# One TRN2 core, a two-part transformer in fp32: where a stage's squares are summed, and where beta is applied

## What is computed

```
def rms_norm(x, w):
    y = x32 * lax.rsqrt(jnp.mean(x32 * x32, axis=-1, keepdims=True) + EPS)
    return (y * w.astype(jnp.float32)).astype(x.dtype)

def gated_delta_rule(q, k, v, g, beta):
    decay = jnp.cumsum(g, axis=-1)
    rel = jnp.exp(jnp.where(causal, decay[..., :, None] - decay[..., None, :], -jnp.inf))
    k_beta = k * beta[..., None]
    a = jnp.where(strict, jnp.einsum('bhnik,bhnjk->bhnij', k_beta, k) * rel, 0.0)
    rhs = jnp.concatenate([v * beta[..., None], k_beta * jnp.exp(decay)[..., None]], axis=-1)
    sol = lax.linalg.triangular_solve(eye + a, rhs, left_side=True, lower=True, unit_diagonal=True)
    ...

def first_block(...):
    for l in range(DEPTH):
        ...
        h = h + rms_norm(xa, norm_xattn_post[l])
        hn = rms_norm(h, norm_ffn_pre[l])
        h = h + rms_norm(swiglu_ffn(hn, w_gate_up[l], w_down[l]), norm_ffn_post[l])
    return h
```

## Time and profile before

| | us |
|---|---|
| median of 3 runs | 2617.42 |
| lowest, highest | 2612.06, 2617.83 |
| the profiled execution's own time | 2612.81 |
| its span in the trace | 2610.9 |
| PE busy | 2529.0 (97%) |
| DVE busy | 1645.3 (63%) |
| ACT busy | 1128.4 (43%) |

### The profile page before, as it was taken

How to read it: one execution, slowest core, us unless ns; L and a number is a source line. 1 busy time by engine, 2 the same in 40 slices (tenths; PEclk the granted TensorE clock), 3 DMA queues, 4 the chain that set the end, 5 groups by cost and what they waited for, 6 DMA issues and landing times.

```text
span 2610.9 us, 34979 instructions
## 1 busy us (share of the span) xinstructions
PE 2529.0 (97%) x13470; PEld 2048.0 (78%) x13470; DVE 1645.3 (63%) x3123; ACT 1128.4 (43%) x2051; POOL 0.2 (0%) x4
## 2 busy tenths in 40 slices
PE   8999999999999999999999999999999999999998
PEld 6878888678888878788986788888876666888666
DVE  6666565364446776665653644478486677499774
ACT  4336444443332243464444433333336667232563
POOL 0000000000000000000000000000000000000000
PEclk9999999999999999999999999999999999999999
DMA  4220043123336522201421222375110000232321
GB/s 164 88 73 17 17 129 105 57 69 109 97 97 224 178 73 93 65 9 41 131 89 62 84 97 98 97 257 174 43 52 14 24 17 17 65 85 64 82 55 49
DMA packets 74083, 219.38 MB, mean 84 GB/s; under 512 B 21312, under 2 KB 21568, under 8 KB 73152
## 3 DMA queue, kind: packets, MB, share of 16 engines
q1 hardware_dynamic: 48384, 176.29, 20.9%
q10 hardware_dynamic: 25536, 40.87, 5.1%
HBM read 215.03 MB, written 2.10 MB: 83 GB/s over the span
## 4 chain that ended last, share of the span: by engine, by line
PE 87%; DVE 7%; ACT 3%; issue 2%; ACTq 0%; DVEq 0%
PE bank L579 21%; PE bank L580 21%; PE bank L581 21%; PE bank L796 4%; PE bank L832 4%; PE bank L806 3%; PE bank L1406 1%; DVE w_lo L545 1%; PE bank L1393 1%; PE bank L698 1%; PE bank L610 1%; PE bank L611 1%; PE bank L612 1%; DVE e_s L897 1%; DVE hT L767 1%
## 5 line engine op out<-in xcount | busy, mean ns | idle before, releaser
L579 PE MATMUL bank<-a_hi,w_hi 128*128 128x512 f32 (+1 forms) x1480 | 591.9, 400 | 19.9 <-DVE w_lo L545 14.5
L538 ACT ACTIVATE w_hi<-w_raw 128x1024 fp32r<-128x1024 f32 x334 | 353.4, 1060 | 562.2 <-PE bank L581 534.2
L581 PE MATMUL bank<-a_hi,w_lo 128*128 128x512 f32 (+1 forms) x1480 | 577.8, 390 | 0.0
L580 PE MATMUL bank<-a_lo,w_hi 128*128 128x512 f32 (+1 forms) x1480 | 577.1, 390 | 0.0
L545 DVE TENSOR_TENSOR w_lo<-w_raw,w_hi 128x1024 fp32r<-128x1024 f32 x334 | 407.7, 1223 | 264.5 <-ACT w_hi L538 263.8
L579 PEld LDWEIGHTS bank<-a_hi,w_hi 128*128 128x128 f32 (+1 forms) x1480 | 276.9, 187 | 88.5 <-issue 14.5
L581 PEld LDWEIGHTS bank<-a_hi,w_lo 128*128 128x128 f32 (+1 forms) x1480 | 276.6, 187 | 60.5
L580 PEld LDWEIGHTS bank<-a_lo,w_hi 128*128 128x128 f32 (+1 forms) x1480 | 277.0, 187 | 57.8 <-issue 1.4
L579 PE MATMUL bank<-b_hi,w_hi 128*128 128x512 f32 x704 | 257.2, 365 | 1.0 <-DVE w_lo L545 0.8
L580 PE MATMUL bank<-b_lo,w_hi 128*128 128x512 f32 x704 | 248.7, 353 | 0.0
L581 PE MATMUL bank<-b_hi,w_lo 128*128 128x512 f32 x704 | 247.5, 352 | 0.0
(11 more groups left out here) (393 smaller groups left out, 3959.2 us busy)
## 6 DMA issues: line engine op xcount, KB each, us to landing
w_raw<-w_tiles SPq DMA_DIRECT2D x334, 512.0 KB, 3.5
mod_raw<-mod_tiles ACTq DMA_DIRECT2D x48, 512.0 KB, 4.2
d_bias<-rpb_rows ACTq DMA_DIRECT2D x16, 224.0 KB, 4.4
hT<-xT ACTq DMA_DIRECT2D x8, 256.0 KB, 6.0
m_in<-memT ACTq DMA_DIRECT2D x2, 1024.0 KB, 4.7
mod_cond<-cond_rows ACTq DMA_DIRECT2D x2, 1024.0 KB, 5.4
out<-hT ACTq DMA_DIRECT2D x8, 256.0 KB, 2.2
ctx_sq<-ctxT ACTq DMA_DIRECT2D x1, 1024.0 KB, 9.1
```

The source lines that it names most:

```text
L538: act.activation(w_hi[:, t % SPLIT, :], w_raw[:, t % RAW, :], ACT.Copy).then_inc(sem("w_rounded"), 1)
L579: pe.matmul(o, wh, hi[:, k, :n], start=k == 0, stop=False)
L580: pe.matmul(o, wh, lo[:, k, :n], start=False, stop=False)
L581: mm = pe.matmul(o, wl, hi[:, k, :n], start=False, stop=k == kc - 1)
```

## The change

Five edits. (1) `last_ssq_pe` goes; `last_product_pe` runs a stage's last product and issues the zero operand and the sums of `sqacc` after the last block but one, so three more product matmuls follow them; only the last chunk's sums stay behind. The `final` stage loses a 512-wide dummy. (2) The one dummy matmul ahead of the row of reciprocals is 256 columns wide instead of 512. (3) ACT takes the root before it rounds the last weight tile. (4) DVE puts the low half of chunk c - 1 ahead of the addition of chunk c, and the low rounding of the last weight tile behind the first addition. (5) Beta is no longer made into a row: the unknowns of the triangular system are scaled so that beta over the squared norm stands in per-token columns (`BR`), which scale k by k on DVE, the k by q copy on ACT and, multiplied into `KD`, the turned k; v is scaled with the norm alone (`VN`). The order of the copies on ACT changes too.

```diff
-            split_lo(dve, last_tile)
             b = bank(dve, "rstd", *post)
             for c in range(KC + 1):
                 if c < KC:
                     post_scale_dve(dve, post, post_gain, y, b, c)
-                    post_add_dve(dve, post, y, c)
                 if c and pre:
                     low_dve(dve, pre, pre_gain, hT, a_hi, a_lo, S, c - 1)
+                if c < KC:
+                    post_add_dve(dve, post, y, c)
+                if c == 0:
+                    split_lo(dve, last_tile)
...
-        def last_ssq_pe(pe, key):
-
-            b = claim(pe, "ssq", *key)
-            pe.matmul(b[:, 0:TT], ident, C("zero").broadcast_to([P, TT]), start=True, stop=True)
-            pe.wait_ge(*when("sq_added", *key, KC - 2))
-            for t in range(TT):
-                pe.matmul(b[:, t:t + 1], sqacc[:, P * t:P * t + P], ones[:, 0:1],
-                          start=False, stop=True, skip_group_check=True)
-            pe.wait_ge(*when("sq", *key, KC - 1))
+        def last_product_pe(pe, key, sums, inputs, kc=KC):
+
+            for k, _ in enumerate(product_steps(pe, key, inputs, kc=kc)):
+                if k == kc - 2:
+                    b = claim(pe, "ssq", *sums)
+                    pe.matmul(b[:, 0:TT], ident, C("zero").broadcast_to([P, TT]), start=True, stop=True)
+                    pe.wait_ge(*when("sq_added", *sums, KC - 2))
+                    for t in range(TT):
+                        pe.matmul(b[:, t:t + 1], sqacc[:, P * t:P * t + P], ones[:, 0:1],
+                                  start=False, stop=True, skip_group_check=True)
+            pe.wait_ge(*when("sq", *sums, KC - 1))
...
-        def gdn_rows_pe(pe, l, n, parts=(0, 1)):
-            for w in parts:
-                pe.wait_ge(*when("g" if w == 0 else "beta_rk2", l))
-                b = claim(pe, "row", l, n, w)
-                column_rows_pe(pe, b, [colnh(GL if w == 0 else BR, n, h) for h in range(GH)],
-                               C("upto") if w == 0 else ident).then_inc(*filled("row", l, n, w))
+        def gdn_rows_pe(pe, l, n):
+            pe.wait_ge(*when("g", l))
+            b = claim(pe, "row", l, n)
+            column_rows_pe(pe, b, [colnh(GL, n, h) for h in range(GH)], C("upto")).then_inc(*filled("row", l, n))
...
-                b = bank(dve, "row", l, n, 1)
-                dve.tensor_tensor(at_mat[:, n, :], rel_t[:, n, :], b[:, :], ALU.mult)\
-                   .then_inc(*freed("row", l, n, 1, also=("beta_rel", l, n)))
-                dve.wait_ge(*when("beta_rel", l, n))
                 b = bank(dve, "kk", l, n)
-                dve.tensor_tensor(at_mat[:, n, :], at_mat[:, n, :], b[:, :], ALU.mult)\
-                   .then_inc(*freed("kk", l, n, also=("a", l, n)))
+                for h in range(GH):
+                    op = dve.scalar_tensor_tensor(out=head(at_mat[:, n, :], h), in0=head(rel_t[:, n, :], h),
+                                                  scalar=colnh(BR, n, h), in1=head(b, h),
+                                                  op0=ALU.mult, op1=ALU.mult)
+                op.then_inc(*freed("kk", l, n, also=("a", l, n)))
...
-                last_ssq_pe(pe, ("x_post", l))
-                warm_pe(pe, 1, "x_rstd", l)
+                last_product_pe(pe, ("x_post", l, KC - 1), ("x_post", l), [("y", a_hi, a_lo, S)])
+                warm_pe(pe, 1, "x_rstd", l, width=2 * P)
```

More of the change, by code:

```diff
@@ L728, in post_norm_act @@
                 act.activation(y[:, c, :], b[:, :], ACT.Copy).then_inc(*freed("y", *key, c, also=("y_in", *key, c)))
-                if after:
+                if after and not (rms and c == KC - 1):
                     after(c)
@@ L1245, in att_take_act, with warm_pe @@
             return take
-        def warm_pe(pe, n, *key):
+        def warm_pe(pe, n, *key, width=512):
             b = claim(pe, "warm", *key)
             for _ in range(n):
-                mm = pe.matmul(b[:, :], ident, con[:, 0:512], start=True, stop=True)
+                mm = pe.matmul(b[:, :width], ident, con[:, 0:width], start=True, stop=True)
             mm.then_inc(*freed("warm", *key))
@@ L1522, in decay_act @@
         def decay_act(act, l, n):
-            b = bank(act, "row", l, n, 0)
+            b = bank(act, "row", l, n)
             act.activation(dec[:, n, :], b[:, :], ACT.Exp).then_inc(*done("dec", l, n))
@@ L1531, in gdn_act, with products, scaled @@
             act.wait_ge(*when("short", l, 1))
-            act.wait_ge(*when("k_decay", l))
-            def scaled(n):
-                b = bank(act, "kt", l, n)
+            act.wait_ge(*when("k_decay_beta", l))
+            def products(n):
+                b = bank(act, "kq", l, n)
                 for h in range(GH):
-                    op = act.activation(head(k_dec[:, n, :], h), head(b, h), ACT.Copy, scale=colnh(KD, n, h))
-                op.then_inc(*freed("kt", l, n, also=("kdec", l, n)))
-                b = bank(act, "kq", l, n)
-                act.activation(attn_t[:, n, :], b[:, :], ACT.Copy).then_inc(*freed("kq", l, n, also=("kq_in", l, n)))
-                b = bank(act, "vt", l, n)
+                    op = act.activation(head(attn_t[:, n, :], h), head(b, h), ACT.Copy, scale=colnh(BR, n, h))
+                op.then_inc(*freed("kq", l, n, also=("kq_in", l, n)))
+            def scaled(name, to, at, event, n):
+                b = bank(act, name, l, n)
                 for h in range(GH):
-                    op = act.activation(head(v_beta[:, n, :], h), head(b, h), ACT.Copy, scale=colnh(VB, n, h))
-                op.then_inc(*freed("vt", l, n, also=("vbeta", l, n)))
+                    op = act.activation(head(to[:, n, :], h), head(b, h), ACT.Copy, scale=colnh(at, n, h))
+                op.then_inc(*freed(name, l, n, also=(event, l, n)))
             def turned(s, n):
@@ L1564, in gdn_act @@
             for n in range(TT):
+                products(n)
+                scaled("kt", k_dec, KD, "kdec", n)
+                if n >= 2:
+                    turned(0, n - 2)
                 if n + 1 < TT:
                     decay_act(act, l, n + 1)
-                scaled(n)
+                if n + 1 == TT:
+                    level(1, n - 3)
+                scaled("vt", v_beta, VN, "vbeta", n)
                 if n + 1 < TT:
                     relative_act(act, l, n + 1)
-                if n >= 2:
-                    turned(0, n - 2)
-                if n >= 3:
-                    level(1, n - 3)
             for n in range(TT - 2, TT):
@@ L2534, in second_pe @@
             group_tiles_pe(pe, [(1, 0), (1, 1)], [("d_y", b_hi, b_lo, S)], inputs_ready(("d_mix",)))
-            for c in range(2, KC):
+            for c in range(2, KC - 1):
                 product(pe, (1, c), [("d_y", b_hi, b_lo, S)])
-            warm_pe(pe, 1, "final_sq")
-            last_ssq_pe(pe, ("final",))
-            warm_pe(pe, 1, "final")
+            last_product_pe(pe, (1, KC - 1), ("final",), [("d_y", b_hi, b_lo, S)])
+            warm_pe(pe, 1, "final", width=2 * P)
             rstd_pe(pe, ("final",), S)
@@ L2797, in ffn_pe @@
                 product(pe, (l, j), [("up_p", a_hi, a_lo, S)])
-            for c in range(KC):
+            for c in range(KC - 1):
                 product(pe, ("f_post", l, c), [("y", f_hi, f_lo, S)], kc=FC,
                         need=inputs_ready(("hid", l)) if c == 0 else None)
-                if l == DEPTH - 1 and c == KC - 2:
-                    ctx_ssq_pe(pe, 0)
+            if l == DEPTH - 1:
+                ctx_ssq_pe(pe, 0)
+            last_product_pe(pe, ("f_post", l, KC - 1), ("f_post", l), [("y", f_hi, f_lo, S)], kc=FC)
         def ffn_dve(dve, l):
@@ L2909, in down_act @@
             rms_act(act, key, S)
+            split_hi(act, first + FC + SPLIT)
             if l == DEPTH - 1:
```

36 lines of the change are left out of this document (19 added, 17 removed).

## The result

| | before | after |
|---|---|---|
| median, us (12 runs each) | 2612.91 | 2620.78 |
| lowest, highest | 2612.06, 2617.83 | 2617.98, 2624.55 |
| the profiled execution: time, span, mean granted clock | 2612.81, 2610.9, 0.994 | 2623.05, 2621.2, 0.986 |

The ratio of after to before is 1.0026, 95% interval 1.0019 to 1.0034: slower by about 7 us. The forecast was 2618.2 with a change of +0.8 us against before. The time lies in the range, 2.6 us above the forecast, but the change itself was 7.9 us in the medians (6.9 in the means of the same runs). Some 2 us of that are waits; the rest goes with a lower granted clock, the matter of rival (a).

A forecast was written before the change was run, and what follows sets the result against it. TensorE, busy through nearly all of the 2610.9 us span, was taken as the bound. Terms 4.8 + 2.0 + 0.4 - 6.4 = +0.8 us on a median of 2617.42 gave 2618.2, range 2609.5 to 2625.

The forecast's parts named there:

- rival (a): TensorE's clock falls to half behind both cross attentions too, adding 3.6 us: 2621.8 us; chance 0.17.
- Set-up, -6.4: Delta rule set-up of both layers: beta on columns gains 3.2 us a layer, -6.4 us.
- Sums, +0.48: Stage's end: sums of squares moved into the last product leave the last squares uncovered, +0.48 us an end.
- Low halves, +1.13: Ends of both cross attentions and first feed-forward: first low half +0.43, then DVE-paced chunks +0.7 us.
- Second feed-forward, +2.0: End of the second feed-forward: the moved weight rounding delays seven of eight additions, +2.0 us.
- Last product, +0.4: Last product's end: sums inside it cost +0.70, the narrower dummy gives 0.3 back, +0.4 us.
- (b): Sums at stage ends hide behind product matmuls and the set-up gains its upper bound: 2612.1 us; chance 0.13.
- (c): Low halves: DVE isn't held by the high half and rounding hides, another -3.5 us: 2608.6; chance 0.05.
- (d): Every chunk where TensorE waits for DVE also costs a restart, 4.2 us; with the clock's fall 2626; chance 0.07.

The follow-up runs named there:

- The new order alone: Kernel before with beta on columns, plus the root ahead of the weight rounding and low halves ahead of the additions; sums and dummies as before: 2613.31 us.

## Why the prediction was right or wrong

**Set-up, -6.4.** Right: -6.25 alone, though in part by luck. The relatives came at 217.16 and 222.40 where I had 216.7 and 221.45, DVE's last operation at 228.77 instead of 227.9, but the way from there to the first update shrank to 3.09 (from 3.93), near the 3.0 that I had counted for a third only. One error of 0.9 and one of 0.5 the other way; the first update is 0.37 later than I had it, and 0.4 of the earliness isn't the set-up's. What I had left out is the half clock near 215 us: it costs about 1.0 in one set-up, and at the full clock a set-up gains 3.4 where I had 3.2.

**Sums, +0.48.** Too small. The measured price of the five instructions inside the product is 1.14 (P moves from 2.49 to 3.63), not 0.95; the last sums are 0.96 later instead of 0.78, the row about 0.75 in after, and with the wide dummy 0.98; the end in all is +1.01 with the wide dummy and 1.85 - 1.02 = +0.83 with the narrow one and the earlier root. These two win back 0.21 in the row where I had 0.30. (My text had eight product matmuls behind the sums; there are three, which changes no term.) The rule of the Trainium skill that I had weighed against the rows (TensorE: Matmul & The Clock Gate, section Step-by-step: what each phase is for), that the next tile's weights load while the present matmul runs, doesn't hide the small ones here when it is taken for all ten instructions: the last product matmul moved by 1.14 us for ten records, 0.11 each.

**Low halves, +1.13.** Right to 0.1: +0.42 (forecast +0.43) at the group's start and +1.02 in all, DVE paces the chunks at 2.15. **Second feed-forward, +2.0:** +2.34. **Last product, +0.4:** +0.7.

Together the waits come to +1.7 to +2.7 instead of +0.8, which by itself would have been within what can't be told from no change.

**The clock.** The step that failed is leaving the clock out of the sum and weighing it as rival (a), with a chance of 0.17 and a price of 3.6 us. In the trace the clock did fall at both cross attentions, twice at each where I had one fall, and these cost 3.8 us together (1.89 and 1.91 above 28.54), near my 3.6. But the first feed-forward lost its fall (-1.6), and 4.7 us more came in work that nobody edited; rival (a) had nothing there. Over all runs the clock's share is about 5.4 us, or 3.6 by before's own slope. The reason that I gave was half wrong: I put the fall on the longer gap behind the row, 2.09 growing to 2.5, and on a new one of 0.8 before the row. The new order alone has that 2.50 us gap and keeps the clock at its three ends. What goes with falls ahead of the group is the thinner piece ahead of the row: 1.03 us of sums taken away from behind the product and an idle gap of 0.69 put in, or half of a dummy gone; each alone is enough (4 of 6 and 6 of 9 ends). My text counted the dummy's loss as a gain only. Why the thinner ends also go with more falls elsewhere stays open.

That the time still lies in the range is luck. The range had been drawn up to 2625, and before's median had been taken from three runs, two of them at 2617.4 and 2617.8; from 12 runs it is 2612.91, and from there the same sum would have given 2613.7, 7 us too low. For the same reason rival (a)'s 2621.8 looks closer than it is: from 2612.91 it would be 2617.3.

Rivals (b), (c) and (d) fell: the sums don't hide, DVE is held by the high half, and no restart cost shows in the chunks (27.71 is 26.69 + 0.42 and about 7 x 0.09).

## What to carry to other kernels

Work of TensorE that lies in the shadow of another engine's step costs nothing there; moved into a product it costs its full length, and it leaves behind a hole. Before such a hole is opened, or a dummy narrowed, ahead of a short latency chain, look at what keeps the granted clock up there, and price a fall of it (here 0.9 us in the chain with the narrow dummy, 1.6 to 2.4 with the wide one, and 1.6 in dense work) at every such place, twice if the chain is long. Then look for falls in work that nobody edited too, by laying the two traces side by side: here they were 4.7 of 10.3 us. When two kernels differ by a few tenths of a per cent, compare their mean granted clock before explaining the difference by waits, from a dozen runs of each and not from three, and try each edit of a bundle alone: here one of five held the whole gain.

## What the runs showed of the hardware

- A matmul with a 128x128 fp32 operand of its own and a single column to move takes 0.22 us of TensorE (four of them, eight records, from 535.35 to 536.25 in after), and the 512-column matmuls ahead of it don't hide it.
- The granted clock fell without any long idle time: behind three dense product matmuls, an idle 0.69 us and the sums, and with the narrow dummy behind sums with no such gap at all. A gap of 2.50 us behind two wide dummies did not bring it down at any of three ends.
- A wide dummy is no free insurance: it takes 0.94 us of the path at the full clock and 1.85 us when the clock is already down, and with the sums inside it did not keep the clock up at 4 of 6 ends.
- The mean granted clock and the time go together from run to run, 1.43 us for each 0.001 over 144 runs, but the slope of a single kernel lies anywhere from 0.95 to 2.86.
